# Expert blocks of 32 rows instead of 64 in a two-layer mixture-of-experts kernel, with their loads and stores on other queues

## What is computed

```python
def moe(x2, w_router, router_bias, w1, w3, w2):      # N = 512 tokens, D = 1024
    expert_idx, gate_w = route(x2, w_router, router_bias)   # 2 of 16 experts a token
    ...                                              # rows sorted by expert, padded to whole blocks
    def run_block(args):
        e, toks = args
        xb = x_pad[toks]
        h = jax.nn.silu(xb @ w1[e]) * (xb @ w3[e])   # w1, w3: 1024 x 512
        return h @ w2[e]                             # w2: 512 x 1024
    yb = lax.map(run_block, (blk_e, slot_tok.reshape(n_blk, MOE_BLOCK)))
    y = yb.reshape(-1, D) * slot_gate[:, None]
    return jnp.zeros((N + 1, D), x2.dtype).at[slot_tok].add(y)[:N]
```

## Time and profile before

| | us |
|---|---|
| median of 3 runs (lowest, highest) | 3765.08 (3765.07, 3767.06) |
| the profiled execution, its own time | 3772.02 |
| its span, first to last instruction | 3770.3 |
| expert part of layer one, first up to last down | 690.6 to 1071.0 |
| expert part of layer two | 1779.7 to 2140.2 |

### The profile page before, as it was taken

One profiled execution on the slowest core, in us unless ns is written; L12 is line 12 of the kernel. 1 busy time (PEld: TensorE's weight loads), 2 busy tenths in 40 slices (PEclk: granted clock), 3 DMA queues, 4 the chain that ended last, 5 costly groups with the idle time before them and its releaser, 6 DMA issues. The chain is left out here.

```text
span 3770.3 us, 45626 instructions
## 1 busy us (share of the span) xinstructions
PE 3506.5 (93%) x15764; PEld 1814.7 (48%) x15764; DVE 1217.8 (32%) x2489; ACT 743.0 (20%) x1389; POOL 178.9 (5%) x169
## 2 busy tenths in 40 slices
PE   8998999799989989997999789999998788899998
PEld 5445444545554454444555334434444677444443
DVE  1564111322233751113322431101457555510102
ACT  1124112222221151112222220000113422100000
POOL 1000002100020000003000110000000000000000
PEclk9999999899989999998999889999999777999999
DMA  7112222798331103224987222245121000122221
GB/s 276 63 45 79 78 78 112 315 385 346 131 134 68 56 23 112 78 106 165 421 348 279 90 69 75 71 95 143 67 76 46 1 0 0 48 75 78 78 78 67
DMA packets 79123, 457.46 MB, mean 121 GB/s; under 512 B 12160, under 2 KB 12296, under 8 KB 32112
## 3 DMA queue, kind: packets, MB, share of 16 engines
q1 hardware_dynamic: 42912, 310.40, 22.0%
q0 software_dynamic: 19776, 112.50, 8.4%
q10 hardware_dynamic: 16272, 32.43, 2.6%
HBM read 416.23 MB, written 39.06 MB: 121 GB/s over the span
## 5 line engine op out<-in xcount | busy, mean ns | idle before, releaser
L890 PE MATMUL pb<-arena,streamed 128*128 128x512 f32 x1408 | 609.6, 595 | 4.8 <-DVE arena L1860 4.1
L800 PE MATMUL pb<-arena,xT 128*64 x1984 | 449.0, 385 | 17.4 <-DVE streamed L1735 7.5
L800 PE MATMUL pb<-streamed,xT 128*64 128x256 f32 x1984 | 449.1, 385 | 0.0
L890 PEld LDWEIGHTS pb<-arena,streamed 128*128 128x128 f32 x1408 | 268.1, 191 | 345.7 <-issue 334.1
L554 PE MATMUL pb<-xT,streamed 128*128 128x512 f32 x832 | 368.0, 601 | 0.0
L800 PEld LDWEIGHTS pb<-arena,xT 128*64 128x64 f32 x1984 | 269.3, 138 | 165.7 <-issue 35.1
L725 PE MATMUL pb<-xT,streamed 128*128 128x512 f32 x768 | 335.4, 595 | 2.5 <-ACT arena L1225 2.5
L916 PE MATMUL pb<-arena,streamed 128*128 128x512 f32 x704 | 306.4, 598 | 9.6 <-DMA streamed<-in_w_tail 7.2
L800 PEld LDWEIGHTS pb<-streamed,xT 128*64 128x64 f32 x1984 | 269.3, 138 | 0.0
L554 PEld LDWEIGHTS pb<-xT,streamed 128*128 128x128 f32 x832 | 159.3, 193 | 200.6 <-issue 200.5
L725 PEld LDWEIGHTS pb<-xT,streamed 128*128 128x128 f32 x768 | 146.3, 191 | 186.7 <-issue 186.7
(11 more groups left out here) (360 smaller groups left out, 3743.4 us busy)
## 6 DMA issues: line engine op xcount, KB each, us to landing
arena<-in_w_moe SPq DMA_DIRECT2D x128, 1024.0 KB, 11.9
streamed<-in_w_tail SPq DMA_DIRECT2D x87, 1024.0 KB, 4.9
streamed<-in_w_layer SPq DMA_DIRECT2D x78, 1024.0 KB, 4.9
arena<-in_w_moe POOLq DMA_DIRECT2D x64, 1024.0 KB, 10.3
ys_dram<-am ACTq DMA_DIRECT2D x120, 128.0 KB, 6.2
xT<-xs_dram ACTq DMA_DIRECT2D x26, 512.0 KB, 7.8
xs_dram<-lnw POOLq DMA_DIRECT2D x16, 512.0 KB, 20.7
lnw<-in_ln_par POOLq DMA_DIRECT2D x4, 1024.0 KB, 5.0
```

The costliest lines, as they stand in the source:

```text
L800: last = mm(pb[m][r0:r0 + MOE_BLOCK, 0:FW], rows, w, start=(k == 0), stop=(k == KC - 1))
L890: last = mm(pb[3 * u + s][:], unit(w, u, k), xn[:, k * S:(k + 1) * S], start=(k == 0), stop=(k == KC - 1))
```

## The change

`MOE_BLOCK` becomes 32, so `COLS` becomes 4, `N_BLK` 47 and the number of 128-row tiles 12 instead of 16. Each matmul of `up` streams 128 columns of weights (256 before), each of `down` 256 (512 before), in four 32-column groups. The relays now hold three quarters of the weights (3072 columns a partition instead of 2048); `w2_relay` moves out of `streamed` into `arena`. TensorE's block loop becomes a hardware loop over groups of four blocks. The table gives each block its expert number instead of three words, and every expert at least one block (a half block is rounded up). GpSimd issues all loads of weights and, having waited for each pair to land, tells the other engines by `expert_here`. SyncE issues the loads of input rows, now one buffer, and the stores of results, one transfer a block, from eight buffers.

```diff
-MOE_BLOCK = 64
+MOE_BLOCK = 32
+Y_BUFS = 8
...
-        w2_relay = streamed[:, 2 * RELAY:3 * RELAY]
+        w2_relay = sr[:, 13312 - S - RELAY:13312 - S]
...
-        def wait_expert(eng, l, values, m):
-
-            for q in range(2):
-                eng.wait_ge(expert_loaded[q][m], l * (16 * N_EXP) + values[1 + q])
-                alone(eng)
+        def block_expert(eng, b):
+
+            return eng.value_load(blk_tab[0:1, N_BLK + b:N_BLK + b + 1], min_val=0, max_val=N_EXP - 1)
...
+                def load_rows(j):
+
+                    sp.wait_ge(xs_tr, l * N_TILE + j)
+                    alone(sp)
+                    sp.dma_start(xs, xs_dram[j * P:(j + 1) * P, :]).then_inc(xs_loaded, 16)
+
+                def store_y(b):
+
+                    if b >= 4:
+                        sp.wait_ge(y_stored[b % 4], 16 * (l * OUT_OF[b % 4] + b // 4) + 1)
+                        alone(sp)
+                    sp.wait_ge(y_copied, l * N_BLK + b + 3)
+                    sp.dma_start(ys_dram[b * MOE_BLOCK:(b + 1) * MOE_BLOCK, :].rearrange("r (g c) -> g r c", g=COLS),
+                                 ysb[b % Y_BUFS]).then_inc(y_stored[b % 4], 16)
...
+                load_rows(1)
+                for b in range(N_BLK - 1):
+                    j = (b + 6) // COLS
+                    if b % COLS == 2 and j < N_TILE:
+                        load_rows(j)
+                    store_y(b)
...
+                def arrived(e, m):
+
+                    pool.wait_ge(expert_loaded[m], (l * N_EXP + e + 1) * 32)
+                    alone(pool)
+                    pool.sem_inc(expert_here[m], 1)
+
...
                 for e in range(2, N_EXP):
...
+                    for m in range(3):
+                        arrived(e - 1, m)
+                        if m < 2:
+                            pool.wait_ge(up_ready, l * (2 * N_BLK) + 2 * end + 1 + m)
+                        else:
+                            pool.wait_ge(y_ready, l * N_BLK + end + 1)
+                        alone(pool)
+                        load(e, 2 * m)
+                        load(e, 2 * m + 1)
...
-                for b in range(1, N_BLK):
-                    ahead = up(b)
-                    if b % COLS == COLS - 1 and b // COLS + 1 < N_TILE:
-                        transpose_xs(b // COLS + 1)
-                    down(b - 1, off)
+                with pe.Fori(0, N_TILE - 1) as i:
+                    off = slot(i * COLS)
+                    for s in range(1, COLS + 1):
+                        b = i * COLS + s
+                        ahead = slot(b)
+                        up(b, s, ahead, i + s // COLS)
+                        if s == COLS - 1:
+                            transpose_xs(i + 1)
+                        down(b - 1, s - 1, off)
+                        turn(b)
+                        off = ahead
...
-                def relay_w1(b):
-
-                    values = block_values(act, b)
-                    wait_expert(act, l, values, 0)
-                    act.wait_ge(up_ready, 2 * (l * N_BLK + b) + 1)
+                def relay_w1(b, e):
+
+                    act.wait_ge(expert_here[0], l * N_EXP + e + 1)
                     alone(act)
...
-                v.tensor_scalar(r_end, r_end, 1.0 / MOE_BLOCK, None, ALU.mult)
+                v.tensor_scalar(r_end, r_end, 1.0 / MOE_BLOCK, 0.5, ALU.mult, ALU.max)
```

More of the change, by code:

```diff
@@ L36 @@
 N_TILE = (N_BLK + COLS - 1) // COLS
-OUT_OF = N_BLK // 2
+Y_BUFS = 8
+OUT_OF = [(N_BLK + 2 - s) // 4 for s in range(4)]
 LAST = (N_BLK - 1) * MOE_BLOCK
-assert N_BLK % 2 == 1 and N_TILE % 2 == 0
+assert COLS == 4 and N_BLK % 4 == 3
 DN_ALPHA = (2 * DEPTH) ** 0.25
@@ L291, in two_blocks @@
         ht_ready, hT_ready, y_ready, y_copied = sem("h_transposed"), sem("hT_ready"), sem("y_ready"), sem("y_copied")
-        y_stored = [sem(f"y_stored{s}") for s in range(2)]
+        y_stored = [sem(f"y_stored{s}") for s in range(4)]
         y_back = [sem(f"y_back{t}") for t in range(NT)]
@@ L477, in _ @@
                 alone(pool)
-                for p in range(UP_PIECES, PIECES):
-                    load_down(1, p)
+                load(1, 3)
+                arrived(0, 2)
+                load(1, 4)
+                load(1, 5)
                 pool.wait_ge(tok_done, 2 * l + 2)
@@ L497, in _ @@
                 for e in range(2, N_EXP):
[L498 to L508, removed]
[L509 to L510 removed]
+                    end = pool.value_load(blk_tab[0:1, 2 * N_BLK + e - 2:2 * N_BLK + e - 1], min_val=0, max_val=N_BLK)
+                    for m in range(3):
[7 more added lines that the diff above has]
+                        load(e, 2 * m + 1)
+                for m in range(3):
+                    arrived(N_EXP - 1, m)
+                for s in range(4):
+                    pool.wait_ge(y_stored[s], 16 * OUT_OF[s] * (l + 1) + 1)
                     alone(pool)
@@ L839, in _ @@
                 turn(0)
-                for b in range(1, N_BLK):
-                    ahead = up(b)
-                    if b % COLS == COLS - 1 and b // COLS + 1 < N_TILE:
-                        transpose_xs(b // COLS + 1)
-                    down(b - 1, off)
+                with pe.Fori(0, N_TILE - 1) as i:
[9 more added lines that the diff above has]
+                        off = ahead
+                off = slot(N_BLK - 3)
+                for s in (1, 2):
+                    b = N_BLK - 3 + s
+                    ahead = slot(b)
+                    up(b, s, ahead, N_TILE - 1)
+                    down(b - 1, s - 1, off)
                     turn(b)
                     off = ahead
-                down(N_BLK - 1, off)
+                down(N_BLK - 1, 2, off)
                 def last_tile(t):
@@ L1160, in _ @@
                 act.dma_start(dst, src).then_inc(loaded, 16)
-            for s in range(2):
+            for s in range(4):
                 act.sem_inc(y_stored[s], 1)
@@ L1810, in _ @@
                 for b in range(N_BLK):
+                    if b + 1 < N_BLK:
+                        ahead = block_expert(dve, b + 1)
                     hidden(b)
@@ L1814, in _ @@
                         alone(dve)
-                    ahead = relay_w3(b + 1) if b + 1 < N_BLK else None
+                    if b + 1 < N_BLK:
+                        relay_w3(b + 1, ahead)
                     if b >= 1:
                         copy_y(b - 1)
-                    relay_w2(b, values)
-                    values = ahead
+                    relay_w2(b, e)
+                    e = ahead
                     if b == 4:
```

161 lines of the change are left out of this document (58 added, 103 removed).

## The result

The changed kernel took **3741.42 us** (median of 4 runs, 3736.41 to 3745.58) against 3765.07 of before on the same chip: a ratio of **0.9937** (95% interval 0.992 to 0.9955), 0.6% faster. The forecast was 3667, with 3720 as its high end. The sign was right; three quarters of the gain are missing.

The account below looks back on a forecast made before the run. TensorE and the transfers stood close before; afterwards transfers set the pace until expert 15 landed. Layers gain 59.6 and 45.7 us, less 7.4 behind the experts: 97.9 off 3772.0 is 3674.1, median 3667; range 3610 to 3720.

Parts of the forecast that it names:

- TensorE's new block: TensorE's up, down, turn and a quarter of a tile transpose for one 32-row block: 5.6 us.
- the 6.7 of an issue limit: TensorE's block at 29 ns a matmul record with unhidden register steps: 6.7 us, kept as the range's upper end.
- rival C: On TensorE, four column groups do not run at once: 10.9 us a block, 284 us slower, 4050; chance 0.05.
- ScalarE's and VectorE's chains: Relays, silu, product, copies, signals and gaps of one block: 5.6 us on ScalarE, 5.2 on VectorE.
- 6.0 us a block: Pace of the expert part's blocks: 0.4 above the longest chain for late relays; 47 blocks are 282 us.
- The transfers at 252 us: A layer's DMA up to the last expert: 223 us of weights by GpSimd's queue plus 29 of rows and stores.
- the stores' pieces halve to 1 KB: Result stores in smaller pieces cost from nothing to twice their share of DMA time: 0 to 13 us.
- The tail behind the experts: After the last block, the gather starts about when the last down ends: 3.7 us a layer lost, 7.4 in all.
- Rival A: In the expert part, blocks at 6.7 us, not transfers, set the pace: 3680, or 3720 with half clock; chance 0.27.
- Rival B: GpSimd issues weight loads too slowly beside VectorE's relays: 5.5 us an expert, 56 slower than before, 3821; chance 0.06.
- Rival D: Nothing to measure: the last expert's weights land as late as before, an 8 us block eats the tail's gain; chance 0.04.
- the forecast's own sign of being wrong: In the loading stretch, a DMA share no higher than the 93% of before while TensorE waits.

Follow-up runs that it names:

- experiment 7: The four-store kernel with weight loads of experts 2 to 15 cut to 1 KB of each 8 KB row: looped 3640.76 us, TensorE's loop written out 3680.25 us.
- four-store kernel: The changed kernel with each block's results stored by four transfers of 32 rows instead of one: 3669.94 us, ratio 0.9749.
- experiment 3: The changed kernel with the loads of input rows moved from SyncE's queue to ScalarE's, stores as changed: 3714.72 us, ratio 0.9869.

## Why the prediction was wrong, point by point

**TensorE's new block: the step right, the sum 0.3 low.** 0.107 us a step; the 6.7 of an issue limit and rival C fall. But the 5.62 us of a block are without a transpose, where the forecast's 5.6 held 0.3 for one: in the looped kernel of experiment 7 TensorE passes from up (3.5 us) to down (1.85) to turn (0.26) and to the next up without a gap:

```profile
759.75 0.29 PE L803 MATMUL pb<-arena,xT 128*32 x1
...
763.26 1.91 PE L826 MATMUL pb<-arena,am 128*32 x32
765.11 0.33 PE L810 MATMUL pb<-cst,am 128*128 128x128 f32 x1
765.37 0.29 PE L803 MATMUL pb<-arena,xT 128*32 x1
```

**ScalarE's and VectorE's chains: right.** 2.77 for w1's relay (2.8 forecast), 1.78 for w3's (1.8), 0.95 as the mean of w2's two copies (0.7 and 1.2), a gap of 0.19 (0.15).

**6.0 us a block: 0.24 low**, 47 blocks, 11 us a layer, and near by luck. The 0.4 above the sum stood for relays that come late, and undisturbed blocks wait for none. In its place stand the 0.3 that the sum lacked and the jump of the loop, 1.3 us for four blocks, which was in no term.

**The transfers at 252 us: right, once they can run.** In the four-store kernel (core's times in us, busy time of PE, PEld, DVE, ACT, POOL, granted clock, DMA share, GB/s):

```profile
713.00:830.00 117.00, 101.86 (x2744) 81.12 (x2740) 71.13 (x88) 59.27 (x58) 35.78 (x42) 1.00 0.98 398
830.00:944.00 114.00, 104.64 (x2866) 83.89 (x2858) 72.30 (x87) 64.38 (x65) 31.22 (x38) 1.00 1.00 407
944.00:1010.00 66.00, 60.83 (x1594) 47.45 (x1594) 41.82 (x53) 30.20 (x32) 1.20 (x2) 0.98 0.16 45
```

100% at 407 GB/s until 944, and 66 us behind it: the forecast's own signs, 400 GB/s until about 950 and 60 us. Its parts of 323.3 and 319.2 are 2.5 and 4.4 above the forecast's, its time 3670 against 3667. But the margin is thin: with an eighth of the weights the blocks need 304 and 307, so the two resources stand within 6% of each other, and the transfers hold TensorE for 19 and 12 us a part and not all the way until expert 15 has landed. Most of its blocks there go at their own 5.62 and 6.85 us.

**The failed step: "the stores' pieces halve to 1 KB, which no row prices; from nothing to twice their share, 0 to 13 us".** It priced the right instruction by the wrong property. Stores in 1 KB pieces go at 3669 us when flat. The shape cost some 70 us: 71.5 between the medians of the changed kernel and four stores, 31.0 and 39.4 in the two parts. And it looked for the price in the engines' busy time, where there was none to be seen; it was paid in waiting. Some 27 us went with the row loads behind held stores in SyncE's queue (experiment 3), the rest, as the rows of experiment 3 have it, mostly with DMA engines that stood idle and weights that landed up to 30 us late (971.3 and 976.2 against 946.6). The prediction named no one who waits behind a held store, though the row loads had been moved to that queue by the same diff, it took the engines' whole rate of 0.395 MB a us as given whatever the stores did, and it did not ask how late a store may be.

**The tail behind the experts: near.** In the four-store kernel the gather starts at 1008.49 and the last record of a down at 1009.7, "about at the end".

**Rival A** is not what happened, though its 3720 was the nearest number: blocks are 6.24 us, not 6.7, and what slowed them was late rows and late weights. Of the clock it was half right: after the 11.07 us of idle time the granted clock was 0.50 from 930 to 934, some 2 us lost (an estimate: 4 us at half the rate). **Rival B** falls: GpSimd issued all pairs and the DMA engines stood at 100%. A pair took 1.05 us where VectorE's copy ended 0.2 us into it, and 2.21 us where a relay of w3 ran beside it (the last line is VectorE's):

```profile
919.91 1.32 POOL L455 DMA_DIRECT2D arena<-in_w_moe  x2 [6.38 <-PE pb L825]
922.06 1.05 POOL L455 DMA_DIRECT2D arena<-in_w_moe  x2 [0.82 <-PE pb L802]
923.81 2.21 POOL L455 DMA_DIRECT2D arena<-in_w_moe  x2 [0.70 <-PE pb L802]
...
924.05 1.85 DVE L1730 COPY streamed<-arena 128x3072 f32 x1 [0.28 <-issue]
```

So what the Trainium skill says in "SBUF — State Buffer", section "SBUF: two separate sides", of VectorE's copies locking GpSimd out fits the 1.2 us between 1.05 and 2.21, but the engines did not run dry of it here: they stood at 100% from 830 to 944. **Rival D** had the last pair of weights issued as late as before, which came true (960.79), for a reason that did not; and the forecast's own sign of being wrong, a DMA share no higher than before while TensorE waits, is what was seen.

## What to carry over

When a diff reshapes a transfer, look at its outermost dimension in both patterns before its bytes or its count of pieces, and write down who stands behind it in its queue and how many buffers' time it has to land. Splitting or merging transfers is no matter of overhead alone: here the same bytes in the same 1 KB pieces cost some 70 us more on a dimension of 4 than on one of 128 or 32. And a hardware loop is to be judged together with the number of instructions in its body and how fast they are used up, not by the price of its jump; the version with four stores and the four-block body, 3670 us, is 1.9% faster than the changed kernel and 2.5% faster than the one before.

## What the runs showed of the hardware that was not expected

- A store with an outermost dimension of 4 held SyncE's own issue for up to 11.6 us, and the next load of rows for up to 13.0; the same store with one of 128 issued in 0.32 us each time. While such stores were about, the DMA engines stood at 0.88 to 0.91 where they reach 0.99 without them.
- TensorE's back jump left 1.17 us of idle time in layer one and 1.34 in layer two where the body has four blocks of 32 rows, and none with four blocks of 64 rows. With eight blocks of 32 rows the program is slower than with no loop at all (3881 against 3850), with idle times of up to 8.0 us at the start of an up.
- A written-out program that uses 320 TensorE instructions in 6.2 us is slower than its loop by 180 us when weights fill the DMA engines, and by 40 us when they stand at 29%; at 160 in 11.4 us a loop makes no difference (ratio 0.9995).
- Four column groups of 32 rows run as fast together as two of 64 do: 128 columns in all four in 0.107 us.
